# Three merges of a two-block transformer: per branch four gates and four products twice, or eight gates and then eight products

## The chip, the cores and the metric

The kernel runs on one core of a Trainium2 chip. Its time is the device time of one execution, in microseconds (us). The core's engines are TensorE (PE in the profile, its weight loads PEld), VectorE (DVE), ScalarE (ACT), GpSimd (POOL) and SyncE (SP), which issues the loads of the weight stream. Each engine runs its own list of instructions in order; they meet only by semaphores.

## What is computed

Two transformer blocks, one after the other, on 256 tokens of width 1024, in float32. The parts that matter are the merges of the branches. The first block merges four branches of width 1024:

```python
gates = jax.nn.sigmoid(proj("gates").reshape(b, s, N_BRANCH, D_MODEL) + b_gate[l])
projected = jnp.einsum('bsnc,ncd->bsnd', branches, w_branch[l])
mixed = jnp.sum(gates * projected, axis=2)
x = x + mixed @ w_out[l]
```

The second block has two layers, and each merges three branches of width 512 (neighbourhood attention, differential attention, gMLP). Its first layer carries 256 tokens of x and 256 of the context together, 512 columns; its last layer only the 256 of x:

```python
def branch_merge(ya, yb, yc, gates, w_branch, w_out):
    ga, gb, gc = jnp.split(jax.nn.sigmoid(gates), N_BRANCH_2, axis=-1)
    m = ga * (ya @ w_branch[0]) + gb * (yb @ w_branch[1]) + gc * (yc @ w_branch[2])
    return m @ w_out
```

Behind each layer of the second block comes a mixture of 16 experts whose weights stream past.

## The kernel before

Activations lie with features on partitions and tokens in columns. A dense projection makes one output chunk of 128 features in one PSUM bank, by the sum over eight (or, in the second block's products, four) input chunks. The weights arrive as one stream in **pieces** of 128 x 1024 numbers, two to a slot of a ring of six (`ring`). Float32 is multiplied in split form: `split_hi` (L498, on ACT) rounds a piece to its high part, `split_lo` (L507 on VectorE, L509 on POOL) subtracts to get the low part, and `three` (L605 to L607) does three matmuls per block, high by high, high by low and low by high. A piece gives 24 matmuls. Which pieces' low parts POOL makes is a table, `GPS_LOW`. Both halves of the split run up to `AHEAD` = 3 pieces in front of TensorE, held back by the `piece_used` semaphores; in program text they hang on `next_piece`, which every engine calls as it passes a piece (`split_ahead`).

The program is a list of stages with a `barrier` between them (L485, semaphore `stage_done`): every engine drains, signals, and waits for four signals. POOL makes its low parts in `lows`, in the stage in which ACT made the high parts.

A **merge** (`merge_pe`, `merge_act`, `merge_dve`) goes branch by branch. ACT rounds the branch's y (L1816) and VectorE subtracts (L1848); TensorE waits for that (`y_lo`) before its first product. Then, for each half h of the eight output chunks: TensorE makes four gate banks, from the activations in `A`, and four product banks, from y in `WKR`. ACT turns each gate bank into `GATE` by a sigmoid (L1820); VectorE multiplies `GATE` with each product bank (L1857) and adds it into `MIXT` (L1859). `GATE` has room for four chunks of 512 columns, so at the start of every half ACT waits for `gate_used`, which VectorE gives, after a drain, at the end of a half. A first-block piece makes one bank of either kind; in the second block a piece makes one gate bank or two product banks. Banks come from a ring of six in the first merge and of eight in the others. In the first merge conditioning steps (`ada_pe`, L2019) on unsplit pieces follow every second piece.

At the end of a merge the mix itself is split for the out projection (`out_pe`): ACT makes the high part of a chunk (`mix_hi_act`, L1800), POOL the low part (`mix_lo_pool`, L1805), and the first bank of the out projection takes all eight chunks in turn, waiting for each. In the last half of the last branch ACT does chunks 0 to 3 right behind the gates and chunks 4 to 7 as VectorE finishes them.

Ahead of a second-block merge lies the gMLP stage. It ends with transposes on TensorE, copied by ACT (`gmlp_mix_act`, L2279); then ACT loads the table for the sigmoid (`table`, L1035: a tiny activation that makes the load happen), and the barrier follows. The stage's gelu is L2230. Before it lies the differential attention (`att_pe`, `att_act`, `att_dve`), during which the gMLP's projections and the splits of the first merge pieces are made; L944 is VectorE's weighting of the two attention maps. Ahead of the first merge lies memory attention, `mem_att`, in two rounds.

## Time and profile before

| | before |
|---|---|
| time, median of 3 runs | 2789.27 us (2784.52 to 2792.49) |
| time of the profiled execution | 2788.38 us |
| its span | 2786.4 us |
| TensorE busy | 2534.9 us |
| VectorE busy | 1044.3 us |
| ACT busy | 880.5 us |
| POOL busy | 424.2 us |
| high parts of pieces (L498) | 378, 393.1 us |
| low parts on VectorE (L507) | 255, 316.5 us |
| low parts on POOL (L509) | 123, 312.7 us |
| mean granted clock of TensorE | 0.98 of full |

The busy times are sums over the whole span; each engine's work lies partly beside the others'. A wait costs time only where TensorE, or the stream of expert weights that later fills the span, stands still for it. So the table says how much work there is, and the rows below say where it is waited for.

### The profile page before, as it was taken

To read this page: it belongs to the slowest core of one execution; us is meant where nothing else is said; L and a number is where in the kernel's file an instruction comes from. 1 tells how busy PE (TensorE), PEld (TensorE's weight loads), DVE (VectorE), ACT (ScalarE), POOL (GpSimd) and SP (SyncE) were. 2 spreads that over 40 slices of the span, in tenths; PEclk is the share of its full clock that TensorE was granted. 3 is DMA by queue.
4 is the path that set the end of the run, shared out by engine and by line. 5 is a ranking of instruction groups with operands and counts; after the bars stand their busy time and mean duration, and the time that the engine had idled before them with its cause. 6 is when DMAs were issued, how large, how long until landed. Compare 5 with 4: busy or idle time off the path is not lost.

```text
span 2786.4 us, 36544 instructions
## 1 busy us (share of the span) xinstructions
PE 2534.9 (91%) x15220; PEld 1805.0 (65%) x15220; DVE 1044.3 (37%) x1528; ACT 880.5 (32%) x1392; POOL 424.2 (15%) x222
## 2 busy tenths in 40 slices
PE   7999989999999999899999888888999998987787
PEld 7888878899998777688863222224777895322223
DVE  4548532326764444544441011113474653000001
ACT  4465544344444344422331100002344442000001
POOL 1430016771001232100220000000133011000000
PEclk9999999999999999899999999999999999999999
DMA  5434327764544221323269999999213448999997
GB/s 211 157 137 153 119 77 280 299 240 174 185 156 152 76 72 46 151 91 121 96 265 397 429 428 429 429 429 377 101 61 133 152 151 361 425 429 429 429 430 316
DMA packets 66510, 668.27 MB, mean 240 GB/s; under 512 B 7328, under 2 KB 8496, under 8 KB 10544
## 3 DMA queue, kind: packets, MB, share of 16 engines
q1 hardware_dynamic: 64368, 655.48, 59.2%
q0 software_dynamic: 1984, 10.51, 1.0%
q8 instruction: 121, 1.98, 0.3%
q14 instruction: 37, 0.30, 0.0%
HBM read 664.89 MB, written 1.06 MB: 239 GB/s over the span
## 4 chain that ended last, share of the span: by engine, by line
PE 54%; DMA 22%; DVE 5%; ACT 3%; issue 2%; PEld 2%; POOL 1%; DVEq 0%; POOLq 0%; PEldq 0%; ACTq 0%
PE ps L605 12%; PE ps L607 12%; PE ps L606 12%; DMA ring<-in_blocks 10%; PE ps L2508 9%; DMA hi_place<-in_blocks 7%; DMA WK<-in_blocks 5%; PE ps L825 1%; PE ps L2019 1%; PE ps L794 1%; POOL A L1805 1%; PE ps L633 1%; PE ps L811 1%; PE ps L613 1%; ACT WK L869 1%
## 5 line engine op out<-in xcount | busy, mean ns | idle before, releaser
L605 PE MATMUL ps<-A,piece_hi 128*128 128x256 f32 (+1 forms) x1952 | 617.8, 316 | 19.7 <-ACTq L485 7.2
L606 PE MATMUL ps<-A,piece_hi 128*128 128x256 f32 (+1 forms) x1952 | 605.2, 310 | 0.0
L607 PE MATMUL ps<-A,ring_lo 128*128 128x256 f32 (+1 forms) x1952 | 604.7, 310 | 0.0
L498 ACT ACTIVATE piece_hi<-ring 128x1024 fp32r<-128x1024 f32 x378 | 393.1, 1053 | 202.0 <-DVEq L644 104.8
L509 POOL TENSOR_TENSOR ring_lo<-ring,piece_hi 128x1024 fp32r<-128x1024 f32 x123 | 312.7, 2554 | 680.2 <-ACT piece_hi L498 622.5
L605 PEld LDWEIGHTS ps<-A,piece_hi 128*128 128x128 f32 x1952 | 377.4, 193 | 58.2 <-issue 24.7
L507 DVE TENSOR_TENSOR ring_lo<-ring,piece_hi 128x1024 fp32r<-128x1024 f32 x255 | 316.5, 1246 | 253.7 <-ACT piece_hi L498 253.2
L606 PEld LDWEIGHTS ps<-A,piece_hi 128*128 128x128 f32 x1952 | 377.9, 194 | 17.8
L607 PEld LDWEIGHTS ps<-A,ring_lo 128*128 128x128 f32 x1952 | 377.5, 193 | 18.1
L2659 DVE TENSOR_TENSOR A_place<-A_place,ps 128x512 f32<-128x512 f32 x32 | 22.0, 688 | 539.4 <-PE ps L2508 539.4
L1047 POOL TENSOR_TENSOR WK<-WK 128x512 f32<-128x512 f32 (+1 forms) x36 | 40.5, 1125 | 1025.5 <-ACT WK L1041 1024.8
L605 PE MATMUL ps<-WKR,piece_hi 128*128 128x256 f32 (+1 forms) x624 | 188.1, 302 | 1.0 <-DVE WKR L726 0.8
L606 PE MATMUL ps<-WKR,piece_hi 128*128 128x256 f32 (+1 forms) x624 | 186.7, 299 | 0.0
L607 PE MATMUL ps<-WKR,ring_lo 128*128 128x256 f32 (+1 forms) x624 | 186.7, 299 | 0.0
L2625 ACT ACTIVATE A_place<-ps 128x512 f32<-128x512 f32 x32 | 19.1, 597 | 495.9 <-PE ps L2508 495.9
L2508 PE MATMUL ps<-ring,A_place 128*64 128x512 f32 x672 | 152.2, 597 | 18.7 <-ACT A_place L2631 13.0
L2508 PE MATMUL ps<-ring,WK 128*64 128x512 f32 x656 | 148.3, 596 | 19.5 <-DMA ring<-in_blocks 19.5
L605 PE MATMUL ps<-piece_hi,A 128*128 128x256 f32 (+1 forms) x480 | 156.2, 325 | 2.5 <-DVE WK L2121 2.3
L607 PE MATMUL ps<-piece_hi,A 128*128 128x256 f32 (+1 forms) x480 | 152.9, 318 | 0.0
L606 PE MATMUL ps<-ring_lo,A 128*128 128x256 f32 (+1 forms) x480 | 152.8, 318 | 0.0
L2508 PE MATMUL ps<-WK 128*64 128x512 f32 x512 | 116.0, 596 | 24.6 <-DMA WK<-in_blocks 24.6
L2608 DVE COPY WK<-ps 32x512 f32<-32x512 f32 x48 | 32.7, 682 | 260.0 <-PE ps L2508 259.8
(295 smaller groups left out, 3283.6 us busy)
## 6 DMA issues: line engine op xcount, KB each, us to landing
ring<-in_stream SPq DMA_DIRECT2D x237, 1024.0 KB, 4.9
ring<-in_blocks SPq DMA_DIRECT2D x82, 2048.0 KB, 25.1
WK<-in_blocks SPq DMA_DIRECT2D x39, 2048.0 KB, 25.6
extra<-in_blocks SPq DMA_DIRECT2D x28, 2048.0 KB, 25.6
hi_place<-in_blocks SPq DMA_DIRECT2D x28, 2048.0 KB, 25.6
A_place<-in_blocks SPq DMA_DIRECT2D x11, 2048.0 KB, 34.6
WK<-in_na_bias POOLq DMA_DIRECT2D x2, 2048.0 KB, 8.0
WK<-in_blocks SPq DMA_DIRECT2D x4, 1024.0 KB, 28.3
```

What stands on the lines that cost most here:

```text
L498: nc.scalar.activation(piece_hi[:, no % 4, :], ring[:, slot, at:at + PIECE], ACT.Copy).then_inc(hi_done[no % 4], 1)
L507: nc.vector.tensor_tensor(to, of, hi, ALU.subtract).then_inc(lo_done[no % 4], 1)
L509: nc.gpsimd.tensor_tensor(to, of, hi, ALU.subtract).then_inc(lo_done[no % 4], 1)
L605: nc.tensor.matmul(out_, l[0], r[0], start=first, stop=False)
L606: nc.tensor.matmul(out_, l[0], r[1], start=False, stop=False)
L607: return nc.tensor.matmul(out_, l[1], r[0], start=False, stop=last)
L613: nc.tensor.matmul(out_.rearrange("p (a t) -> p a t", a=2), ident, ident.unsqueeze(1).to_broadcast([P, 2, P]), start=True, stop=True)
L633: last = nc.tensor.matmul(ps[0:rows, b, at:at + n], l, r, start=(k == 0), stop=(k == len(pairs) - 1))
L794: last = nc.tensor.matmul(dst[:, a, qt, :], l, m, start=(j == 0), stop=(j == len(pairs) - 1))
L1047: ins = nc.gpsimd.tensor_tensor(sq[:, 0, 0:n], sq[:, 0, 0:n], sq[:, c, 0:n], ALU.add)
L2508: last = nc.tensor.matmul(ps[64 * n:64 * n + 64, bank, :].rearrange("p (a t) -> p a t", a=2), lhs, block_half(pe, layer, b, k % 4, n), sta ...
L2608: return copy(YE[row:row + CAP, s, e // 4 % 2, half * 512:half * 512 + 512], ps[64 * half + CAP * s:64 * half + CAP * (s + 1), 6 + e % 2, :])
```

## The change

In all three merges a branch now does its eight gates and then its eight products. The order of the weight stream follows, as do the three engines' programs. The room for gates doubles: with 256 columns both halves fit in `GATE`, with 512 a second place, `LATER_GATE`, is used. ACT waits for `gate_used` once per branch, and before it splits chunks 0 to 3 of the mix. Beside this:

- the table load for the sigmoid comes ahead of the gMLP copies (`table` before `gmlp_mix_act`);
- `GPS_LOW` has the first three merge pieces of both layers of the second block, before only those of the first layer;
- memory attention puts its products into banks 0 to 3 instead of 6 and 7;
- a table `GATES_AHEAD` allows gates ahead of a merge; all its values are 0.

```diff
+GATES_AHEAD = {"first": 0, 0: 0, 1: 0}
...
-                   (block + 32, block + 35)):
+                   *((block + l * layer + 32, block + l * layer + 35 + GATES_AHEAD[l]) for l in range(LAYERS))):
...
-                if at["y_bank"] < 6:
+                if at["y_bank"](r) == 4:
                     pe.wait_ge(att_saved, CREDIT + base + r)
...
-            return (YT[:, 3, 4 * r:4 * r + 4, :].rearrange("p (b c) t -> p b (c t)", b=2), ps[:, 6:8, :])
+            return (YT[:, 3, 4 * r:4 * r + 4, :].rearrange("p (b c) t -> p b (c t)", b=2), ps[:, 2 * r:2 * r + 2, :])
...
+        LATER_GATE = wk(16640, 4, 2 * T)
...
+        def gate_at(n, h, j):
+
+            if n == T:
+                return GATE[:, j, h * T:(h + 1) * T]
+            return (GATE, LATER_GATE)[h][:, j, :]
...
             for i in range(branches):
-                for h in range(2):
-                    for _ in range(2):
-                        two_pieces(in_a()(n), DC)
-                    if h == 0:
-                        pe.wait_ge(y_lo, cur.base("y") + 1 + i)
-                    for _ in range(kc // 4):
-                        two_pieces(lambda k: (yh[:, k, :], yl[:, k, :]), kc)
+                for _ in range((8 - (0 if i else ahead)) // 2):
+                    two_pieces(in_a()(n), DC)
+                pe.wait_ge(y_lo, cur.base("y") + 1 + i)
+                for _ in range(2 * kc // 4):
+                    two_pieces(lambda k: (yh[:, k, :], yl[:, k, :]), kc)
...
+            for i in range(branches):
+                act.wait_ge(gate_used, cur.base("merge") + 1 + i * 2)
+                nc.scalar.activation(yh, y[:, i, :, 0:n], ACT.Copy).then_inc(y_hi, 1)
+                for c in range(0 if i else ahead, DC):
+                    gate_act(act, cur, i, c, n, bias)
                 for h in range(2):
...
                     last = (i, h) == (branches - 1, 1)
                     if last:
+                        act.wait_ge(gate_used, cur.base("merge") + 2 + i * 2)
                         for c in range(4):
                             mix_hi_act(c, n)
...
+                for _ in range((8 - (0 if i else ahead)) // 2):
+                    skip_fm(dve, cur, 2)
+                    behind_two()
+                gates_end = cur.g
                 for h in range(2):
-                    for _ in range(2):
-                        skip_fm(dve, cur, 2)
-                        behind_two()
-
-                    dve.wait_ge(bank_free[cur.bank(cur.g - 1)], cur.bank_use(1, cur.g - 1))
+                    if h == 0:
+                        dve.wait_ge(bank_free[cur.bank(gates_end - 1)], cur.bank_use(1, gates_end - 1))
...
-                gmlp_mix_act(act, cur, n // P)
                 table(steps, ACT.Sigmoid)
+                gmlp_mix_act(act, cur, n // P, layer)
                 barrier(act, cur)
```

The first place is ACT at the end of the gMLP stage of the second block's first layer. In these rows L2279 and L2308 are the copies, L1035 and L1039 the table, L1816 and L1831 the first operation of the merge. Before:

```order
L498 ACTIVATE piece_hi<-ring 128x1024 [waits piece_used3,landed5]
L498 ACTIVATE piece_hi<-ring 128x1024 [waits piece_used0,landed0]
L2279 ACTIVATE WK<-ps 128x4x128 [waits bank_full3]
L2279 ACTIVATE WK<-ps 128x4x128 [waits bank_full4]
L2279 ACTIVATE WK<-ps 128x4x128 [waits bank_full5]
L2279 ACTIVATE WK<-ps 128x4x128 [waits bank_full0]
L1035 ACT_TABLE_LOAD
L1035 ACTIVATE idle<-idle 128x1
L1816 ACTIVATE WKR<-WK 128x2048 [waits act_step,gate_used,stage_done]
```

And with the change:

```order
L501 ACTIVATE piece_hi<-ring 128x1024 [waits piece_used3,landed5]
L501 ACTIVATE piece_hi<-ring 128x1024 [waits piece_used0,landed0]
L1039 ACT_TABLE_LOAD
L1039 ACTIVATE idle<-idle 128x1
L2308 ACTIVATE WK<-ps 128x4x128 [waits bank_full3,act_step]
L2308 ACTIVATE WK<-ps 128x4x128 [waits bank_full4]
L2308 ACTIVATE WK<-ps 128x4x128 [waits bank_full5]
L2308 ACTIVATE WK<-ps 128x4x128 [waits bank_full0]
L1831 ACTIVATE WKR<-WK 128x2048 [waits gate_used,stage_done]
```

The load moved from behind the four copies to ahead of them; there is still one load.

The second place is ACT in the last branch of that layer's merge. L1820 and L1824 are sigmoids of gate banks, L498 and L501 high parts of pieces, L1800 and L1812 high parts of the mix. Before:

```order
L1820 ACTIVATE WK<-ps 128x512 [waits bank_full2]
L498 ACTIVATE piece_hi<-ring 128x1024 [waits piece_used1,landed4]
L1820 ACTIVATE WK<-ps 128x512 [waits bank_full3]
L498 ACTIVATE piece_hi<-ring 128x1024 [waits piece_used2,landed5]
L1800 ACTIVATE A<-WK 128x512 x4
L498 ACTIVATE piece_hi<-ring 128x1024 [waits piece_used3,landed5]
L1800 ACTIVATE A<-WK 128x512 [waits bank_free4]
```

And with the change:

```order
L1824 ACTIVATE WK<-ps 128x512 [waits bank_full7]
L501 ACTIVATE piece_hi<-ring 128x1024 [waits piece_used0,landed4]
L501 ACTIVATE piece_hi<-ring 128x1024 [waits piece_used1,landed4]
L501 ACTIVATE piece_hi<-ring 128x1024 [waits piece_used2,landed5]
L1812 ACTIVATE A<-WK 128x512 [waits gate_used]
L1812 ACTIVATE A<-WK 128x512 x3
L501 ACTIVATE piece_hi<-ring 128x1024 [waits piece_used3,landed5]
L1812 ACTIVATE A<-WK 128x512 [waits bank_free4]
```

The last gates lie four product banks further back, and the first high part of the mix has got a wait for `gate_used`.

The third place is POOL's whole order in the last layer, up to the split of the mix (L1805, L1817). L509 and L512 are low parts of pieces. Before:

```order
L509 TENSOR_TENSOR ring_lo<-ring,piece_hi 128x1024 x15
L3192 DMA WK<-in_w_s 128x512
L3193 DMA WK<-in_ln_g 128x512
L3194 DMA WK<-in_ln_b 128x512
L509 TENSOR_TENSOR ring_lo<-ring,piece_hi 128x1024 x5
L1805 TENSOR_TENSOR A<-WK,A 128x256 x8
```

And with the change:

```order
L512 TENSOR_TENSOR ring_lo<-ring,piece_hi 128x1024 x15
L3224 DMA WK<-in_w_s 128x512
L3225 DMA WK<-in_ln_g 128x512
L3226 DMA WK<-in_ln_b 128x512
L512 TENSOR_TENSOR ring_lo<-ring,piece_hi 128x1024 x8
L1817 TENSOR_TENSOR A<-WK,A 128x256 x8
```

Three low parts have come to POOL's list ahead of the gMLP stage; VectorE's list has three fewer.

## Rows read from the trace of the kernel before

**Rows 1.** The table by stretch, one row per merge of the program.

```profile
413.67:634.70 221.03, 219.88 (x1774) 196.19 (x1774) 73.14 (x78) 89.49 (x109) 159.28 (x70) 0.99 0.72 266
1179.42:1385.00 205.58, 204.58 (x889) 168.79 (x890) 89.71 (x88) 60.34 (x72) 14.26 (x8) 0.99 0.29 103
2174.43:2285.00 110.57, 109.01 (x885) 108.13 (x885) 68.08 (x88) 50.71 (x72) 8.96 (x8) 0.98 0.49 172
```

**Rows 2.** TensorE's waits over the span (us, times, longest), then timeline at merges' edges.

```profile
PE ps L605 <- ACTq L485: 7.2, 3, 2.7
PE ps L605 <- POOL A L1805: 3.6, 5, 1.0
...
1179.42 0.79 PE L605 MATMUL ps<-A,piece_hi 128*128 128x512 f32 x1 [2.24 <-ACTq L485]
1384.13 0.50 PE L605 MATMUL ps<-A,piece_hi 128*128 128x512 f32 x1 [1.00 <-POOL A L1805]
2174.43 0.39 PE L605 MATMUL ps<-A,piece_hi 128*128 128x256 f32 x1 [2.24 <-ACTq L485]
```

**Rows 3.** Groups by line in the first merge, then ACT's timeline near its end.

```profile
L509 POOL TENSOR_TENSOR ring_lo<-ring,piece_hi 128x1024 fp32r<-128x1024 f32 x61 | 150.2, 2479 | 91.1 <-ACT piece_hi L498 91.0
L1859 DVE TENSOR_TENSOR WK<-WK 128x256 f32<-128x256 f32 x32 | 41.4, 1293 | 1.1
L1816 ACT ACTIVATE WKR<-WK 128x2048 fp32r<-128x2048 f32 x4 | 7.7, 1914 | 12.9 <-DVEq L1863 10.5 <-DVEq L1844 2.4
...
616.23 0.47 ACT L1820 ACTIVATE WK<-ps,par 128x256 f32<-128x256 f32 x1 [1.46 <-PE ps L607]
619.11 0.47 ACT L1820 ACTIVATE WK<-ps,par 128x256 f32<-128x256 f32 x1 [1.46 <-PE ps L607]
```

**Rows 4.** Timeline of VectorE in the last merge, two successive product pieces.

```profile
2190.32 0.42 DVE L1857 TENSOR_TENSOR WK<-WK,ps 128x256 f32<-128x256 f32 x1
...
2193.04 0.42 DVE L1857 TENSOR_TENSOR WK<-WK,ps 128x256 f32<-128x256 f32 x1
```

**Rows 5.** Timeline of ACT at the end of the two gMLP stages.

```profile
1174.11 0.60 ACT L2279 ACTIVATE WK<-ps 128x512 f32<-128x512 f32 x1 [8.66 <-PE ps L631]
...
1177.83 1.28 ACT L1035 ACT_TABLE_LOAD   x1
...
2172.84 1.28 ACT L1035 ACT_TABLE_LOAD   x1
```

**Rows 6.** The table by stretch, the first 4 us of the second merge.

```profile
1179.40:1183.40 4.00, 3.98 (x9) 3.14 (x10) 3.11 (x1) 0.00 (x0) 0.00 (x0) 0.50 0.00 0
```

**Rows 7.** Timelines of VectorE and ACT, differential attention of the last layer.

```profile
2136.31 3.53 DVE L944 SCALAR_TENSOR_TENSOR WK<-WK,small 128x512 f32<-128x512 f32 x2
...
2149.29 1.41 DVE L944 SCALAR_TENSOR_TENSOR WK<-WK,small 128x512 f32<-128x512 f32 x2
...
2155.34 1.05 ACT L498 ACTIVATE piece_hi<-ring 128x1024 fp32r<-128x1024 f32 x1
...
2158.27 1.15 ACT L2230 ACTIVATE WK<-WK 128x512 f32<-128x512 f32 x2
```

**Rows 8.** Timelines of ACT, VectorE and POOL at the ends of both later merges.

```profile
1367.61 0.60 ACT L1820 ACTIVATE WK<-ps 128x512 f32<-128x512 f32 x1 [3.89 <-PE ps L607]
...
1369.18 1.23 DVE L507 TENSOR_TENSOR ring_lo<-ring,piece_hi 128x1024 fp32r<-128x1024 f32 x1 [4.21 <-ACT piece_hi L498]
...
1369.81 14.26 POOL L1805 TENSOR_TENSOR A<-WK,A 128x512 fp32r<-128x512 f32 x8 [193.58 <-ACT A L1800]
...
2275.99 8.96 POOL L1805 TENSOR_TENSOR A<-WK,A 128x256 fp32r<-128x256 f32 x8 [133.91 <-ACT A L1800]
```

**Rows 9.** Timelines of VectorE, POOL and ACT, last branch of the first merge.

```profile
605.19 2.52 DVE L1859 TENSOR_TENSOR WK<-WK 128x256 f32<-128x256 f32 x1
...
620.61 4.97 POOL L509 TENSOR_TENSOR ring_lo<-ring,piece_hi 128x1024 fp32r<-128x1024 f32 x2 [0.47 <-ACT piece_hi L498]
...
621.65 2.00 ACT L498 ACTIVATE piece_hi<-ring 128x1024 fp32r<-128x1024 f32 x2
```

More of the change, by code:

```diff
@@ L142, in steps @@
                     ADA_LAST[ada_step(part, slot)[:2]] = at - 1
-    steps(0, range(32), 2)
+    at += GATES_AHEAD["first"]
+    steps(0, range((64 - GATES_AHEAD["first"]) // 2), 2)
     at += BLOCK_PIECES - 22 * 4 - 64
@@ L824, in product @@
                         for rows, col, pairs in parts[at_:at_ + width]:
-                            last = nc.tensor.matmul(ps[rows, at["y_bank"] + col // 512, col % 512:col % 512 + T], *pairs[j],
+                            last = nc.tensor.matmul(ps[rows, at["y_bank"](r) + col // 512, col % 512:col % 512 + T], *pairs[j],
                                                     start=(j == 0), stop=(j == kc - 1))
@@ L2204, in build, with gates_ahead_of_tile @@
         GST = wk(18688 + 1536, 4, 8)
+        def gates_ahead_of_tile(layer, m, tt):
+            n = GATES_AHEAD[layer]
+            return (m + 1) * n // tt - m * n // tt
         def gmlp_pe(pe, cur, tt, layer, lam_init):
@@ L2887, in _ @@
             cur.set_ring(range(6))
-            merge_pe(pe, cur, 4, DC, T, ada=0)
+            merge_pe(pe, cur, 4, DC, T, GATES_AHEAD["first"], ada=0)
             cur.set_ring(range(NB))
@@ L2925, in _ @@
                 cur.set_ring(range(NB))
-                merge_pe(pe, cur, 3, BC, n)
+                merge_pe(pe, cur, 3, BC, n, GATES_AHEAD[layer])
                 out_pe(pe, cur, n)
@@ L2992, in _ @@
             cur.set_ring(range(6))
-            merge_act(act, cur, 4, DC, T, YT, lambda i, c: p1("b_gate", i * DC + c))
+            merge_act(act, cur, 4, DC, T, YT, GATES_AHEAD["first"], lambda i, c: p1("b_gate", i * DC + c))
             cur.set_ring(range(NB))
@@ L3087, in _ @@
             cur.set_ring(range(6))
-            merge_dve(dve, cur, steps, 4, DC, T, YT, ada=0)
+            merge_dve(dve, cur, steps, 4, DC, T, YT, GATES_AHEAD["first"], ada=0)
             cur.set_ring(range(NB))
@@ L3273, in _stream @@
     tm(x["w_mem_kv"][0], D, 2 * D)
+    two = -(GATES_AHEAD["first"] // 2)
     for n in range(4):
-        for h in range(2):
-            for j, w, at in ((0, w_in, g0 + n * D), (1, w_in, g0 + n * D), (2, x["w_branch"][0, n], 0), (3, x["w_branch"][0, n], 0)):
-                at += h * 512 + j % 2 * 256
-                fm(w, at, at + 256)
-                ada(0, 8 * n + 4 * h + j)
+        for w, at in ((w_in, g0 + n * D), (x["w_branch"][0, n], 0)):
+            for j in range(4):
+                fm(w, at + j * 256, at + j * 256 + 256)
+                if two >= 0:
+                    ada(0, two)
+                two += 1
     fm(x["w_out"][0], 0, D)
```

64 lines of the change are left out of this document (38 added, 26 removed).

## The prediction, made before the changed kernel was run

> **What bounds the kernel now.** The change removes no matmul, so it pays only where TensorE stands still. First the table by stretch: the three merges lie at 413.67 to 634.7, 1179.42 to 1385.0 and 2174.43 to 2285.0 us, and TensorE is busy for 219.88 of 221.03, 204.58 of 205.58 and 109.01 of 110.57 us of them [rows 1]. Then the list of TensorE's waits over the whole span: the split matmuls of L605 waited three times for ACT at a stage's end, 7.2 us, and five times for POOL's low parts of the mix, 3.6 us [rows 2]. The timeline puts 2.24 us before each second-block merge and 1.00 us at the end of the first of these two [rows 2]; the first merge's start has the other 7.2 - 4.5 = 2.7 us. Between gates and products, or from branch to branch, there is no wait at all. So what the edit reorders is covered, and all it can win at the merges' edges is 7.2 + 3.6 = 10.8 us, 0.39% of 2788.38. I take 0.3%, 8.4 us, as what a measurement of this kernel can tell from no change.
>
> **Part 1: gates and products.** The counts stay: per branch eight gates and eight products on TensorE, eight sigmoids on ACT, eight multiplies and adds on VectorE, the same pieces of weights in a new order of the stream. At 256 columns a piece takes 619.11 - 616.23 = 2.88 us, the distance of two gates [rows 3]. Removed are ACT's wait and VectorE's hand-over between the halves; both lie under TensorE's work, 0 us. What covers them is the splitting of weights ahead: ACT makes a piece's high part up to three pieces early, and POOL or VectorE its low part.
> In the first merge POOL takes 2.48 us a piece, and 61 low parts fill 150.2 of 221 us [rows 3]: it keeps up in either order. In the last merge VectorE has low parts and products: the pairs of multiply and add of two banks and one low part go round in 2193.04 - 2190.32 = 2.72 us [rows 4], under 2.88, so it does not fall behind in four product pieces in a row either. With 512 columns a piece lasts about twice as long. Cost 0 us; the upper bound is rival B.
>
> **Part 2: the sigmoid table ahead of the copies.** ACT idles 8.66 us before its gMLP copies, then copies, then loads the table, and only then reaches the stage's end. The load starts at 1177.83 and TensorE at 1179.42; in the last layer 2172.84 and 2174.43 [rows 2, 5]. With the load inside the idle time TensorE starts about 0.1 us after the last copy: 1.59 - 0.1 = 1.5 us won, twice, **-3.0 us**. Bounds: 0, should the load come again for the first sigmoid or another engine hold the stage, and -3.0.
> The Trainium skill, page "ScalarE: Activation LUTs", section "What ACT_TABLE_LOAD costs", puts a switch to another set at 1.28 us for the load and 1.38 us of draining, 2.66 us together. By that the two would give 5.3 in place of 3.0 and the sum would be 2.3 us lower. The trace agrees with 1.28 for the load and shows TensorE started 1.59 after the load began, so no such drain is there to win.
>
> **Part 3: the clock at these starts.** From 1179.4 to 1183.4 the granted clock was 0.50, the 1.2 GHz level, after TensorE had stood still [rows 6]; 4 us at half speed cost 2 us. A shorter gap may keep the clock up (-2, and as much in the last layer), or only shift the fall (0). Nothing in the rows says at what point of the gap it fell, so I take 0 and keep both ends.
>
> **Part 4: three low parts go from VectorE to POOL in the last layer.** They are the first three merge pieces, made during the differential attention; POOL's order has 8 low parts there in place of 5. ACT's last high part starts at 2155.34 and ends at 2156.39. POOL's low part of 2.48 us then ends at about 2158.9, and POOL must reach that stage's end before ACT's gelu can start, which it did at 2158.27 [rows 7]. Cost **+0.6 us**. Bounds: 0, and +2.1: beside POOL's low parts VectorE's pair of L944 took 3.53 us, alone 1.41 [rows 7], and TensorE turns the result of that chain. Against it VectorE is rid of low parts of 1.23 us ahead of the same chain, so I take the first value, the nearest row.
> The Trainium skill, page "GPSIMD Engine Reference", section "1. Specifications", says that GpSimd and VectorE share SBUF interfaces and contend when a VectorE instruction has two SBUF inputs. The rows of L944 agree. By that rule alone this part would cost 2.1 us and the sum be 1.5 higher.
>
> **Part 5: the end of each merge.** This is the part that can cost. ACT rounds chunks 0 to 3 of the mix, POOL subtracts, and the first bank of the out projection needs all eight. Before, ACT did it right behind the last gate's sigmoid and a high part. Now, at the same point of TensorE's work, it waits for `gate_used`, which VectorE gives after its fourth product and the low part queued behind that. So the price is (multiply and add, low part, hand-over) less (sigmoid, high part).
> Second merge: POOL made its eight subtractions without a pause in 14.26 us from 1369.81, and TensorE waited 1.00 us for the last [rows 2, 8], so POOL's start sets the end. Before: sigmoid 0.60 and high part 1.05, less their overlap, 1.5. Now: a pair at 256 columns is half of 2.72 - 1.23, 0.75, so 1.4 or so at 512, then 1.23 and 0.1, 2.7. **+1.2 us**.
> Last merge, 256 columns: before 0.47 at most and 1.05, about 1.4; now 0.75 + 1.23 + 0.3 = 2.3. POOL again ran without a pause, from 2275.99 [rows 8]. **+0.9 us**.
> First merge: POOL first finishes two low parts, begun at 620.61, the second from a high part that was ready at about 622.7 [rows 9]. In the new order products don't hold ACT, the earlier of the two comes a piece sooner, and POOL waits for the second alone: it begins at 622.7 in place of 620.61 + 2.48 = 623.1. **-0.4 us**.
> Bounds: 0 for each of the three, and twice the value, or +1 for the first.
>
> **Part 6: memory attention's banks.** Its products go to banks 0 to 3 in place of 6 and 7; all its waits remain, and those banks' scores are read by then. 0 us. `GATES_AHEAD` is zero for all three merges, so the code for gates ahead issues nothing.
>
> **Sum:** -3.0 + 0 + 0.6 + 1.2 + 0.9 - 0.4 = **-0.7 us** against the profiled execution's 2788.38 (span 2786.4), which is 0.9 below the median of 2789.27; on the median 2788.6 us. All favourable ends: -3.0 - 4.0 + 0 + 0 - 0.8 = -7.8. All unfavourable: 0 + 0 + 2.1 + 2.4 + 1.8 + 1.0 = +7.3. Independent parts don't all fall one way; about half of each, -4.5 and +4.
>
> **Rivals.**
> A, faster: the edges close, clock included. For it speaks that the clock was at half at the second merge's start. If parts 2 and 3 give all (-7.0) and TensorE's waits for POOL go too (-3.6), with part 4 at +0.6, it is -10.0: 2779.3. Against it: the chain at the merges' ends gets longer, not shorter. 6%.
> B, slower: VectorE falls behind in the eight products of the first merge, and the next branch starts late. POOL's low parts do hold VectorE's adds: one took 2.52 us, and the mean is 1.29 [rows 3, 9]. From TensorE's last product to the low part of the next branch's fourth piece the chain is multiply 0.42, add 2.52, copy of y 1.91, sigmoid 0.47, high part 1.05, low part 2.48 [rows 3, 4, 7, 9], 8.85 us, and TensorE needs 3 x 2.88 = 8.64 for three gates. It decides where VectorE is a whole further piece behind, 2.9 us. At one and a half, 4.3, three starts lose 4.3 + 0.2 each, 13.5 us: 2802. Against it: 0.42 + 2.52 = 2.94 is only 0.06 over a piece even at the worst. 8%.
> C, the change does not do at the edges what it says: the table is loaded again, or POOL holds the stage. Part 2 gives 0, -0.7 + 3.0: 2791.6. 8%.
> D, the clock stays up at one or both starts: -2 to -4 more, 2784.6 to 2786.6. 8%.
> The forecast has the remaining 70%.
>
> **How the numbers follow.** The forecast, C and D lie within 8.4 us of 2789.3: 86% for the same; A is the 6% for faster, B the 8% for slower. The runs shown spread from 2784.52 to 2792.49 around their median, and I allow 1.5 us for a median of such runs. Range: 2788.6 - 4.5 - 1.5 = 2782.6, and 2788.6 + 4 + 1.5 = 2794, to 2795 for the nearest part of B. It takes in C and D and leaves out A and B, 14%.
>
> **What would show it.** Part 2: ACT's table load ahead of the gMLP copies, and the merge's first matmul 1.5 us sooner after the last copy. Part 4: POOL's low part ends after 2158.27, measured from ACT's last high part, and the gelu follows it. Part 5: a wait near 2 us in place of 1.00 behind the second merge. A wait of L605 inside a merge would mean B. The forecast is wrong if the merges' edges keep their waits and the time still moves, or if waits appear where now there is none.

## The result and the profile after

The changed kernel took 2792.99 us (median of 20 runs, 2790.73 to 2795.41), the kernel before 2788.35 in 20 runs on the same chip: ratio 1.0017, 95% interval 1.001 to 1.0023. So it is slower, by 2.8 to 6.4 us, where 0.7 us less was forecast. The profiled execution has a span of 2790.8 us against 2786.4.

First TensorE's waits in the changed kernel, by releaser (us in total, times, longest), which answer to [rows 2]:

```profile
PE ps L1240 <- ACT WK L1261: 5.9, 2, 4.9
PE ps L608 <- POOL A L1817: 4.8, 9, 1.2
PE ps L608 <- ACTq L488: 4.1, 3, 2.7
```

And the wait for the gelu's chain (two of them, the last layer's is the longer) in the kernel before:

```profile
PE ps L1236 <- ACT WK L1257: 5.4, 2, 4.1
```

The merges' starts lost 7.2 - 4.1 = 3.1 us of waits, as forecast. The waits at the merges' ends grew by 4.8 - 3.6 = 1.2 us (1.0, 1.0 and 1.6 at the three ends before, 1.5, 1.5 and 1.7 now), and the wait for the gelu's chain in the last layer 4.9 - 4.1 = 0.8. The waits named here come to -3.1 + 1.2 + 0.8 = -1.1 us, so none of the 4.4 us of the spans is explained by them. The table by stretch tells more: columns are the stretch, its length, busy time of TensorE, its weight loads, VectorE, ACT and POOL, then TensorE's granted clock (1.00 is the 2.4 GHz level), DMA share and GB/s. In the changed kernel, the three merges, then 3.4 us behind the first merge's end and 3.3 behind the second's:

```profile
415.09:635.84 220.75, 219.23 (x1768) 195.52 (x1768) 68.61 (x78) 89.88 (x109) 157.89 (x68) 0.99 0.72 267
1181.24:1385.00 203.76, 202.24 (x889) 166.69 (x890) 89.12 (x88) 60.48 (x72) 13.89 (x8) 1.00 0.29 104
2178.66:2288.00 109.34, 107.53 (x885) 106.51 (x885) 67.78 (x88) 50.83 (x72) 8.15 (x8) 1.00 0.49 174
637.00:640.40 3.40, 3.33 (x16) 3.25 (x16) 1.55 (x2) 1.37 (x2) 0.78 (x2) 0.51 0.46 140
1384.70:1388.00 3.30, 3.30 (x10) 2.54 (x9) 2.00 (x3) 1.58 (x2) 0.00 (x0) 0.51 0.00 0
```

And the same two places of the kernel before:

```profile
635.60:639.00 3.40, 3.40 (x31) 3.40 (x30) 2.09 (x4) 1.90 (x3) 0.00 (x0) 1.00 0.75 292
1385.00:1388.30 3.30, 3.30 (x16) 2.72 (x15) 2.01 (x3) 1.58 (x2) 0.00 (x0) 1.00 0.00 0
```

The bodies of the merges are as before [rows 1], with no new wait between or inside branches. But behind both ends the granted clock is now 0.51, about 1.2 GHz: TensorE starts 16 matmuls in the time of 31, and 10 in the time of 16, and stays "busy" all the while. Such stretches let its busy time grow, from 2534.9 to 2539.1 us in all, at the same 15220 matmuls. Behind the last merge it is the other way round. The kernel before, then the changed one:

```profile
2284.30:2287.70 3.40, 3.38 (x15) 3.29 (x16) 1.54 (x2) 1.37 (x2) 0.65 (x1) 0.53 0.00 0
```

```profile
2288.15:2291.55 3.40, 3.33 (x28) 3.26 (x28) 1.61 (x2) 1.37 (x2) 0.08 (x1) 1.00 0.02 5
```

**A ledger over all profiles.** Every kernel of this study runs those 15220 matmuls in the same stages, so the time between the starts of the same two of them (counted from the first) compares kernels, waits and clock together. In us; "body" stretches inside the merges are alike in all (212.4, 185.87, 93.60) and left out. The columns: up to the first merge's start (1st to 2631st matmul); its end (4361st to 4401st); from there past the second merge's start (to 7961st); the second merge's end (8781st to 8861st); layer 0's experts and layer 1's attention (to 12281st); past the last merge's start (to 12421st); from the last merge's end on (13201st to the last; it has the last merge's end in it). The names other than before and after are the kernels below.

| kernel | begin | 1st end | 2nd start | 2nd end | between | last start | rest |
|---|---|---|---|---|---|---|---|
| before | 407.70 | 6.71 | 557.13 | 19.47 | 755.16 | 31.53 | 501.46 |
| before_again | 406.83 | 6.75 | 553.69 | 19.47 | 755.17 | 31.52 | 502.20 |
| after | 408.90 | 9.22 | 552.19 | 21.87 | 757.63 | 30.40 | 503.10 |
| after_again | 409.64 | 9.23 | 552.43 | 21.90 | 757.12 | 30.41 | 501.26 |
| banks_back | 407.85 | 9.13 | 552.39 | 21.91 | 757.21 | 30.41 | 503.50 |
| low_back | 409.92 | 9.11 | 552.36 | 21.92 | 757.79 | 28.29 | 502.39 |
| table_only | 412.24 | 6.73 | 551.24 | 19.47 | 757.62 | 31.23 | 502.01 |
| order_only | 412.22 | 9.11 | 555.60 | 20.30 | 756.19 | 33.03 | 501.85 |
| high_first | 409.72 | 5.55 | 551.53 | 20.29 | 757.56 | 30.18 | 506.41 |
| late_round | 411.82 | 6.71 | 553.60 | 21.21 | 753.82 | 31.89 | 504.75 |
| chunk_first | 411.49 | 5.55 | 553.83 | 20.29 | 754.40 | 30.42 | 501.83 |
| chunk_second | 410.79 | 9.22 | 552.47 | 18.13 | 758.00 | 32.61 | 504.30 |
| chunkwise | 406.92 | 5.56 | 552.24 | 18.13 | 754.47 | 30.41 | 502.02 |
| chunk_low | 410.22 | 5.59 | 551.59 | 18.13 | 756.36 | 31.27 | 502.20 |

The mean of the two profiles of the changed kernel, less the mean of the two of before: begin +2.0, 1st end +2.5, 2nd start -3.1, 2nd end +2.4, between +2.2, last start -1.1, rest +0.4; together +5.3, near the 4.6 of the medians. The first end repeats within 0.15 us where nothing touches it. The second end takes one of two values at the same waits: about 21.9 with a fall of the clock behind it, 20.3 without. The outer columns swing by several us from one execution to the next: "begin" lies between 406.83 and 412.24 in before, before_again, table_only and late_round, which are one program up to there. So a single profile can't carry a verdict there.

Two places that the wide columns hide, counted in the same way: the second merge's first matmuls (7911th to 7961st) and the last merge's end (13201st to 13290th).

| kernel | second merge's start | last end |
|---|---|---|
| before | 14.28 | 14.84 |
| before_again | 14.24 | 14.85 |
| after | 11.45 | 14.13 |
| after_again | 11.45 | 14.11 |
| table_only | 13.36 | 14.94 |
| order_only | 13.07 | 14.82 |
| chunkwise | 11.44 | 13.69 |

With these the ledger parts as follows. Where the change acts, the changed kernel is not slower in these profiles: 1st end +2.5, 2nd end +2.4, last end -0.7, second merge's start -4.3 (1.5 of wait and 2.8 of clock), last start -1.1, together -1.2. The other +6.5 us lie where it changes little or nothing: begin +2.0, between the first end and the second merge +1.2, between +2.2, behind the last end +1.1. Two profiles of each kernel can't tell how much of that is swing. So that the ends got dearer is plain in the ledger; that they are what makes the whole kernel slower has to come from the experiments.

### The profile page after: what moved, and what is told of

It is laid out like the page before. It is cut to its first block, busy times and chain, and to the rows that moved or that the text cites. A ratio compares the mean times of both kernels' runs of the same rounds, so it can differ in the third digit from the quotient of the medians.

```text
span 2790.8 us, 36540 instructions
## 1 busy us (share of the span) xinstructions
PE 2539.1 (91%) x15220; PEld 1806.0 (65%) x15220; DVE 1037.5 (37%) x1525; ACT 881.4 (32%) x1392; POOL 431.4 (15%) x225
## 4 chain that ended last, share of the span: by engine, by line
PE 53%; DMA 22%; DVE 6%; ACT 3%; issue 2%; PEld 2%; POOL 2%; DVEq 0%; POOLq 0%; PEldq 0%; ACTq 0%
PE ps L608 12%; DMA WK<-in_blocks 12%; PE ps L610 12%; PE ps L609 12%; DMA ring<-in_blocks 10%; PE ps L2537 9%; PE ps L2035 1%; PE ps L797 1%; PE ps L828 1%; POOL A L1817 1%; PE ps L636 1%; PE ps L814 1%; ACT WK L872 1%; PE ps L616 1%; DVE small L933 1%
## 5 line engine op out<-in xcount | busy, mean ns | idle before, releaser
L501 ACT ACTIVATE piece_hi<-ring 128x1024 fp32r<-128x1024 f32 x378 | 393.8, 1054 | 229.6 <-DVEq L647 126.6
L512 POOL TENSOR_TENSOR ring_lo<-ring,piece_hi 128x1024 fp32r<-128x1024 f32 x126 | 320.8, 2557 | 689.9 <-ACT piece_hi L501 632.8
```

Of the source, the lines that this page charges most:

```text
L501: nc.scalar.activation(piece_hi[:, no % 4, :], ring[:, slot, at:at + PIECE], ACT.Copy).then_inc(hi_done[no % 4], 1)
L512: nc.gpsimd.tensor_tensor(to, of, hi, ALU.subtract).then_inc(lo_done[no % 4], 1)
```

## What holds the merges' ends

**The first merge.** ACT and then POOL in the changed kernel at its end:

```profile
617.68 1.06 ACT L501 ACTIVATE piece_hi<-ring 128x1024 fp32r<-128x1024 f32 x1 [1.82 <-DVEq L647]
623.28 1.34 ACT L1812 ACTIVATE A<-WK 128x256 fp32r<-128x256 f32 x4 [4.54 <-DVEq L1879]
624.52 1.99 ACT L501 ACTIVATE piece_hi<-ring 128x1024 fp32r<-128x1024 f32 x2
...
610.51 12.40 POOL L512 TENSOR_TENSOR ring_lo<-ring,piece_hi 128x1024 fp32r<-128x1024 f32 x5 [0.47 <-ACT piece_hi L501]
625.64 2.42 POOL L512 TENSOR_TENSOR ring_lo<-ring,piece_hi 128x1024 fp32r<-128x1024 f32 x1 [2.73 <-ACT piece_hi L501]
628.00 9.11 POOL L1817 TENSOR_TENSOR A<-WK,A 128x256 fp32r<-128x256 f32 x8
```

ACT stands 4.54 us at its wait for `gate_used` (L1879 gives it). Queued behind that wait is the high part of the piece whose low part is POOL's last. POOL therefore stands 2.73 us and starts the eight subtractions of the mix at 628.00. In the kernel before:

```profile
625.54 9.09 POOL L1805 TENSOR_TENSOR A<-WK,A 128x256 fp32r<-128x256 f32 x8
```

Against TensorE's position that is 628.00 - 1.42 - 625.54 = 1.0 us later than before (1.42 us is how late the changed kernel was at the 4321st matmul).

**The second merge.** TensorE's two longest waits there, and POOL:

```profile
1382.75 0.50 PE L608 MATMUL ps<-A,piece_hi 128*128 128x512 f32 x1 [1.25 <-POOL A L1817]
1383.98 0.50 PE L608 MATMUL ps<-A,piece_hi 128*128 128x512 f32 x1 [0.27 <-POOL A L1817]
...
1370.04 13.89 POOL L1817 TENSOR_TENSOR A<-WK,A 128x512 fp32r<-128x512 f32 x8 [190.47 <-ACT A L1812]
```

The changed kernel was 1.0 us ahead here, so POOL started 1370.04 + 1.0 - 1369.81 = 1.2 us later, which is the forecast's number. The clock's fall behind it was not in the forecast.

## The experiments

Four were made first, to part the change into its pieces and mend the place suspected.

**table_only**, the kernel before with one line moved:

```
+                table(steps, ACT.Sigmoid)
                 gmlp_mix_act(act, cur, n // P)
-                table(steps, ACT.Sigmoid)
```

> The kernel before, with nothing changed but the sigmoid table's load put ahead of the gMLP copies. Theory 1 (the change wins at the starts of the second-block merges and loses more at the merges' ends): TensorE's three waits for ACT's queue go from 7.2 us to about 4.1, the ends keep 3.6 us of waits for POOL, and the granted clock at the start of the second merge stays up as in the changed kernel, 1.7 to 3.4 us more: 3.0 to 6.4 us below the kernel before, ratio 0.9977 to 0.9989. Theory 2 (the table move itself does harm, or its gain is given back at the next wait): ratio 0.9995 or more.

2787.56 us against 2789.5: ratio 0.9991 (0.9981 to 1.0). Faster by some 2 us, at the edge of what can be told from nothing, and short of the 3.0 to 6.4 expected. The waits for ACT's queue did go to 4.1. But at the second merge's start the clock did not stay up, as theory 1 had it: it was at half until 4.0 us behind the first matmul, and the start took 13.36 us, against 14.28 before and 11.45 in the changed kernel. So the move of the table alone does not free that start from the half clock. In the last layer the clock took most of the won time back. Around the start, in this kernel (the first matmul of the merge is at 2174.48, 1.6 us into the window) and from the start in the kernel before:

```profile
2172.90:2179.60 6.70, 5.97 (x28) 5.58 (x29) 2.99 (x2) 1.83 (x3) 0.00 (x0) 0.50 0.01 2
```

```profile
2174.43:2178.00 3.57, 3.57 (x20) 3.57 (x21) 1.90 (x2) 1.06 (x1) 0.00 (x0) 0.62 0.02 5
```

TensorE waits 1.5 us less and starts 1.1 us sooner against the 12281st matmul, since the transposes ahead ran at the lower level too; then it spends more of its work at that level, and the column "last start" is only 0.3 us shorter.

**order_only**, the reverse: the changed kernel without the table's move, the three low parts and the banks.

> The kernel before with the order of gates and products changed in all three merges, and neither the table's move, nor the three low parts on POOL, nor the other banks of the memory attention. Theory 1: the waits at the merges' ends are 4.8 us or more, those at their starts 7.2 us again, and the half-clock stretch at the second merge's start is back: 2 to 6 us above the changed kernel, 2795 to 2799. Theory 2 (the order costs nothing; the loss is in the other parts): 2789 to 2790, as the kernel before.

2798.72 us, ratio 1.0036 (1.0023 to 1.0049), from 5 runs. It is 9.2 us slower than the kernel before, twice as much as the whole change; theory 2 is out. The size is not well known: it stands on five runs, and of the 9 us by which the profile is longer, 5 lie in "begin", where the program is that of the kernel before. Its waits are as theory 1 had them, 7.2 and 4.8 us. At the second merge's start the half clock is back, as expected (13.07 us). At its second end the waits alone stand in the ledger: 20.30, 0.83 over the kernel before, with no fall of the clock. With the fall it is 21.9.

**low_back**:

```
-                   *((block + l * layer + 32, block + l * layer + 35 + GATES_AHEAD[l]) for l in range(LAYERS))):
+                   (block + 32, block + 35)):
```

> The changed kernel with the last layer's first three merge pieces given back to VectorE for their low parts. Theory 1: the wait for the gelu's input in the last layer goes from 4.9 back to about 4.1 us, 0.5 to 1.0 us below the changed kernel, 2792 to 2792.5. Theory 2 (this part is what made the kernel slower): 3 to 5 us below it, 2788 to 2790.

2791.5 us, ratio 1.0013 (1.0004 to 1.0023). The gelu's wait is 4.1 again, as theory 1 had it; the time is 1.5 lower than the changed kernel's, a little more than expected and inside the intervals. This part is not the loss.

**chunkwise**, the mend. In the last branch of each merge ACT no longer waits once for four chunks:

```
-                for h in range(2):
-                    last = (i, h) == (branches - 1, 1)
-                    if last:
-                        act.wait_ge(gate_used, cur.base("merge") + 2 + i * 2)
-                        for c in range(4):
-                            mix_hi_act(c, n)
...
+                for c in range(DC):
+                    read_bank(act, cur, False, None, piece=(kc == DC or c % 2 == 1))
+                    if i == branches - 1 and c > 0:
+                        act.wait_ge(bank_free[cur.bank(cur.g - 2)], cur.bank_use(1, cur.g - 2))
+                        mix_hi_act(c - 1, n)
```

> The changed kernel, but in the last branch of each merge ACT rounds each chunk of the mix behind the product piece after it, in place of four chunks behind one wait for VectorE. Theory 1 (the loss sits at the merges' ends): POOL starts its subtractions earlier, TensorE's 4.8 us of waits for POOL's low parts of the mix fall below 1.5 us, and the half-clock stretches of 3.4 us behind the first and the second merge are gone (1.7 us each): 4 to 7 us below the changed kernel, 2786 to 2789. Theory 2 (the loss sits in the last layer's attention, with the three low parts that went to POOL): no more than 2 us below it, 2791 to 2793.

2785.75 us, 7 us under the changed kernel; against before 0.999 (0.9978 to 1.0002). Both ends fall under the kernel before: 5.56 and 18.13. The half-clock rows behind both are gone. Of the waits for POOL 2.7 us are left, more than the 1.5 expected: 0.5 at the first end, none at the second, and 2.2 at the last, where the last chunks' roundings come two by two with a piece between and POOL's last pair is late. Against TensorE's position the last end is still 0.4 us shorter than in the changed kernel (13.69 and 14.13). Theory 2 allowed 2 us at most. Nothing but the rounding at the ends was edited, and the loss was gone; but both ends went below the kernel before, so some of the 7 us was never lost.

Then the same place was taken apart.

**high_first**: in the first merge alone, ACT makes the next high part before that wait.

```
+                    if last and kc == DC:
+                        read_bank(act, cur, False, None, piece=True)
                     if last:
                         act.wait_ge(gate_used, cur.base("merge") + 2 + i * 2)
...
-                        read_bank(act, cur, False, None, piece=(kc == DC or j % 2 == 1))
+                        if not (last and kc == DC and j == 0):
+                            read_bank(act, cur, False, None, piece=(kc == DC or j % 2 == 1))
```

> The changed kernel, but at the end of the first merge ACT makes the high part of the next piece of weights before it waits for VectorE's fourth product, not behind it. Theory 1 (that high part, held behind ACT's wait, leaves POOL idle for 2.73 us before its last low part, and its eight subtractions of the mix start late): POOL's pause falls below 0.6 us, the subtractions start about 2.5 us earlier, TensorE's stretch at the first merge's end is 2.5 us shorter (1.2 of wait, 1.3 of half clock): 2790 to 2791 if the changed kernel is 2793. Theory 2 (POOL's start is set by the roundings themselves): the stretch stays within 0.3 us.

ACT and POOL in this kernel:

```profile
621.52 1.06 ACT L501 ACTIVATE piece_hi<-ring 128x1024 fp32r<-128x1024 f32 x1 [2.10 <-DVEq L647]
623.98 1.34 ACT L1812 ACTIVATE A<-WK 128x256 fp32r<-128x256 f32 x4 [1.40 <-DVEq L1882]
...
611.20 14.97 POOL L512 TENSOR_TENSOR ring_lo<-ring,piece_hi 128x1024 fp32r<-128x1024 f32 x6 [0.48 <-ACT piece_hi L501]
626.12 7.45 POOL L1817 TENSOR_TENSOR A<-WK,A 128x256 fp32r<-128x256 f32 x7
634.38 1.19 POOL L1817 TENSOR_TENSOR A<-WK,A 128x256 fp32r<-128x256 f32 x1 [0.81 <-ACT A L1812]
```

POOL's six low parts now follow one another without the pause. The subtractions start 2.6 us earlier (this kernel was 0.7 us behind the changed one there: 628.00 + 0.7 - 626.12), and the end falls from 9.22 to 5.55 us, by more than the 2.5 expected: one high part held behind one wait was worth 3.7 us at that place, clock included. The whole kernel took 2791.36 us (1.0008, 0.9998 to 1.0018), 1.6 under the changed kernel, a difference that the intervals don't secure; "rest" was 3 to 5 us longer in this profile.

**chunk_first**, the rounding by chunks in the first merge alone (`if kc == DC`):

> The changed kernel with the rounding chunk by chunk in the first merge alone. Theory 1: the stretch at the first merge's end falls by 3.6 us against the changed kernel, as in the kernel with all three (there 1.15 under the kernel before), the second and last merges stay as in the changed kernel: 2789 to 2790.5. Rival (the three ends are not additive, since an end that is mended gives the clock back elsewhere): 2786 or 2792.

2791.03 us, ratio 1.001 (1.0001 to 1.0019): half a microsecond over the range. The first end is 5.55, 3.7 less, as expected. The second was expected as in the changed kernel and is 20.29: the same waits of 1.25 and 0.27 us, but no fall behind them. high_first has 20.29 too. Both kernels differ from the changed one in the first merge alone, so whether the clock falls at the second end is not settled by the waits there.

**chunk_second**, in the two later merges alone (`if kc == BC`):

> The changed kernel with the rounding chunk by chunk in the two second-block merges alone. Theory 1 (the clock falls behind longer waits, and the second merge's end brings the larger part of the lost clock, since with the first merge alone mended the mean granted clock stayed at 0.980): TensorE's stretch at the second merge's end is 3.7 us shorter than in the changed kernel, the mean granted clock is 0.981 or more, 2787 to 2789. Rival (the parts don't show singly; only all three ends together raise the clock): 2790 to 2792 and 0.980.

2788.76 us, ratio 0.9998 (0.9988 to 1.0007), within the expected 2787 to 2789. The ends are 9.22 and 18.13, 3.7 below the changed kernel at the second, as expected. The mean granted clock over its 11 runs is 0.9806, just short of 0.981. The two halves, 2.0 and 4.2 us, come to 6.2 of the 7.2 that all three ends gave.

**late_round**, the kernel before in its own order, with the first four roundings put later:

```
-                    if last:
-                        for c in range(4):
-                            mix_hi_act(c, n)
                     for j in range(4):
                         read_bank(act, cur, False, None, piece=(kc == DC or j % 2 == 1))
+                        if last and j == 0:
+                            act.wait_ge(bank_free[cur.bank(cur.g - 1)], cur.bank_use(1, cur.g - 1))
+                            for c in range(4):
+                                mix_hi_act(c, n)
```

> The kernel before, in its own order of gates and products, but in each merge's last half ACT rounds the first four chunks behind VectorE's first product there, in place of right behind the last gate: the price of a later start of POOL's subtractions, by itself. Theory 1 (a later start is what the reordering costs, and it draws the clock with it): POOL starts 2 to 3 us later at the second and the last merge, TensorE's waits for POOL go from 3.6 to 7 to 9 us, the mean granted clock falls by 0.001 to 0.002, 5 to 9 us above the kernel before, 2794 to 2799. Rival (only the wait counts, the clock does not follow): 2 to 4 us above.

2793.97 us against 2789.21, ratio 1.002 (1.001 to 1.003). POOL started at 1373.39 and 2279.80:

```profile
PE ps L605 <- POOL A L1805: 5.5, 8, 1.2
...
1373.39 13.31 POOL L1805 TENSOR_TENSOR A<-WK,A 128x512 fp32r<-128x512 f32 x8 [196.71 <-ACT A L1800]
```

A late start of POOL alone, in the old order, makes the kernel slower by 4.8 us, about as much as the change did. But neither theory was met: the waits grew by 1.9 and not by 3.4 or more, since POOL went through its eight in 13.31 in place of 14.26 us, and the mean granted clock fell by 0.0005 (0.9820 to 0.9815), no more than the error of its 11 runs. The second end is 1.7 longer and the last end 1.8 (16.67 against 14.85), with no half-clock row right behind the second end.

**banks_back**, memory attention's products in banks 6 and 7 again:

```
-            cur.set_ring((6, 7))
             att_pe(pe, cur, mem_att)
...
-            return (YT[:, 3, 4 * r:4 * r + 4, :].rearrange("p (b c) t -> p b (c t)", b=2), ps[:, 2 * r:2 * r + 2, :])
+            return (YT[:, 3, 4 * r:4 * r + 4, :].rearrange("p (b c) t -> p b (c t)", b=2), ps[:, 6:8, :])
```

> The changed kernel with the memory attention's products in banks 6 and 7 again, as before the change. Theory 1 (this part costs nothing): the stretch up to the first merge keeps its waits and the time is within 1.5 us of the changed kernel, 2791.5 to 2794.5. Rival (the order of the banks costs a wait or a clock fall ahead of the first merge): 2788 to 2790.

2792.7 us, ratio 1.0014 (1.0005 to 1.0023): as the changed kernel. This part costs nothing.

**before_again** and **after_again**, both kernels unchanged for second profiles:

> The kernel before, unchanged, for a second profile of it. Theory 1 (the clock's short falls come at TensorE's waits, but not in the same ones in every execution): the waits at the merges' starts and ends repeat within 0.3 us, and the half-clock stretches differ from the first profile in 3 or more places, most of all in the stages that the change does not touch. Rival (the falls are fixed by the program): the same stretches at the same places. Time 2788 to 2790, ratio 0.999 to 1.001.

2789.87 us, 1.0002 (0.9993 to 1.0012). The waits repeat: 7.2 and 3.6 us at the merges' edges. The clock's falls don't: "2nd start" differs by 3.4 us between the two profiles of one kernel, and the first has several half-clock rows that the second lacks. Over the whole execution the first was granted 0.980 of the clock and the second 0.984.

> The changed kernel once more, for a second profile. Theory 1: 2792 to 2794, mean granted clock 0.980 against 0.982 of the kernel before; half-clock stretches again behind the first and the second merge, other places move. Rival (the first 20 runs were high by chance): 2789 to 2790.5.

2792.65 us, 1.0012 (1.0003 to 1.0022), with the falls behind both ends again (9.23 and 21.90). The slower result is no chance.

**chunk_low**, chunkwise rounding and the three low parts back on VectorE:

> The changed kernel with the rounding chunk by chunk in all three merges, and the last layer's three low parts back on VectorE. Theory 1: the gains add up: the waits at the merges' ends are gone, the gelu's input waits 4.1 in place of 4.9 us, 1.5 to 2 us below the kernel with chunkwise rounding alone, 2783 to 2785, and faster than the kernel before by 3 to 6 us. Rival (below the level of the kernel with only the table moved nothing is left to win): 2786 to 2788.

2782.94 us against 2789.65, ratio 0.9976 (0.9967 to 0.9986): 6.7 us faster than the kernel before and about 10 faster than the change as made. TensorE's waits and POOL at the second merge's end, in this kernel:

```profile
PE ps L1240 <- ACT WK L1261: 4.7, 2, 4.1
PE ps L608 <- ACTq L488: 4.1, 3, 2.7
PE ps L608 <- POOL A L1817: 2.8, 4, 1.0
...
1357.46 1.29 POOL L1817 TENSOR_TENSOR A<-WK,A 128x512 fp32r<-128x512 f32 x1 [181.10 <-ACT A L1812]
1376.46 1.55 POOL L1817 TENSOR_TENSOR A<-WK,A 128x512 fp32r<-128x512 f32 x1 [1.30 <-ACT A L1812]
```

The 2.8 us are 0.5 at the first end, none at the second, 2.2 at the last. In the second merge POOL starts some 9 us earlier against TensorE's position (this kernel was 3.2 us ahead of the changed one there) and is done at 1378.0; TensorE no longer waits for it. The old order can't do this, since the rounded mix goes into the tile that the second half's gates still read. So the new order is an advantage at the ends, once the rounding uses it: the first end is 1.2 and the second 1.3 us shorter than before. The rest of the 6.7 us is not parted; the moved table load is in it too.

## Why the prediction was wrong

The point was 2788.6 and the result 2792.99, in the range, but with the sign against it; "slower by over 0.3%" was not reached either.

**Part 5, the ends of the merges, is the step that failed, and with it the clock, for which the sum had no term behind the ends.** It forecast +1.2 (second), +0.9 (last) and -0.4 (first merge), with bounds of 0 and twice the value, or +1 for the first; together +1.7. Measured from matmul to matmul: +2.4, -0.7 and +2.5, together +4.2. Each parts into waits and clock:

- Second end: 0.8 is waits (20.3 in the three kernels in which the clock did not fall there), 1.6 the clock.
- First end: the lag behind the kernel before grows from 1.42 to 2.47 us up to the 4386th matmul, so the waits and the slow starts behind them cost 1.05; from there on at half clock 1.46 more are lost.
- Last end: the waits cost 0.5 (the 13222nd matmul comes 5.53 us behind the 13201st, before 4.99). POOL started 1.1 us later and took 8.38 us for its eight in place of 8.96 [rows 8]. But the kernel before had a fall of the clock behind this end, in both profiles, and the changed kernel has none.

By waits alone the three come to 2.4 us where 1.7 was forecast. Even that is near by luck: an end forecast as a gain was a loss, and the two others were over-sized (the hand-over in them, 0.1 and 0.3 us, came from no row).

- In the first merge the mechanism itself was wrong. "it begins at 622.7", the forecast said, from a high part that would be ready as before [rows 9]. But ACT's queue is in order: the high part stands behind the new wait for `gate_used`. I had counted that wait's price for the mix and not for what is queued behind it. high_first shows it: that high part put ahead of the wait, and the end is 3.7 us shorter.
- In the second merge the wait was a little over-sized (1.2 for 0.8, since POOL took 13.89 in place of 14.26 us for its eight) and the clock behind it left out. A gap of 1.0 us before [rows 2] left the clock at 1.00; 1.25 and 0.27 us, with smaller ones about them, were followed by 0.51 in four profiles (after, after_again, banks_back, low_back) and not in three (order_only, high_first, chunk_first). The forecast looked at the clock only where TensorE had been still for 2.24 us.

That the rounding at the ends is worth this much is shown by the mends: all three ends edited gave 7.2 us back, the first alone 2.0, the two others 4.2. It is not shown that the ends are the whole loss. In chunkwise the places that the change touches are 9.1 us shorter than before (ends -1.2, -1.3 and -1.2, second start -4.3, last start -1.1), and the kernel gained only 2.8 us by the ratio and 3.8 by the medians. So there as in the changed kernel some 6 us are lost at places that the change leaves alone; which ones and why stays open.

**Part 3, the clock at the starts**, was put at 0 with bounds of -4 and 0. At the second merge's start it is full in all four profiles that keep the unmended change (for instance from 1181.20, below), where it was at half before [rows 6]. That is worth 2.8 us there (14.26 to 11.45), more than the 2 that the bound had, and is what rival D named. Neither the table's move alone (13.36) nor the order alone (13.07) gave it. Yet "2nd start" as a whole fell by 3.1 us on the mean of two, and by 1.3 against before_again: the falls move among stages ahead of it. So D's condition came true at one start, and the time that it forecast did not follow. In the last layer table_only gave most of the won 1.5 back. To "only shift the fall", the other case that the forecast named, is what it did there.

```profile
1181.20:1185.20 4.00, 3.96 (x17) 3.30 (x18) 3.11 (x1) 0.00 (x0) 0.00 (x0) 1.00 0.00 0
```

**Part 2, the table**, held: waits 7.2 to 4.1 us, 1.5 at each start, no second load. The Trainium skill's 2.66 us per switch (page "ScalarE: Activation LUTs", section "What ACT_TABLE_LOAD costs") would have taken 5.3 off; the traces disagree, 3.1 went.

**Part 4, three low parts to POOL**, forecast +0.6, was +0.8 to +0.9 (4.9 against 4.1 in the lists, 4.95 against 4.06 in the timelines): POOL's last low part, and ACT's gelu waiting for POOL. In the changed kernel:

```profile
2160.32 2.34 POOL L512 TENSOR_TENSOR ring_lo<-ring,piece_hi 128x1024 fp32r<-128x1024 f32 x1 [3.78 <-ACT piece_hi L501]
...
2163.02 1.15 ACT L2253 ACTIVATE WK<-WK 128x512 f32<-128x512 f32 x2 [0.90 <-POOLq L488]
```

With the clock it is more in place ("last start" is 2.1 us shorter in low_back), but the whole kernel gained 1.5 at most by undoing it.

**Part 1 and part 6** held at 0: the bodies of the merges agree to 0.1 us, so rival B, VectorE falling behind in eight products, did not occur, and banks_back is as the changed kernel. Rival C failed with part 2. Rival A did not occur; chunk_low reached 6.7 of its 10.0 us, with a mend that A did not name.

**The clock as a whole.** The mean granted clock over all timed runs is 0.9801 for the changed kernel (20 runs, and 10 more) and 0.9817 to 0.9820 for the kernel before (29 and twice 33 runs). One less the clock, times the time, is what TensorE would make up at full clock if it were always busy: 2793 x 0.0199 = 55.6 against 2789 x 0.0183 = 51.0 us. The difference, 4.6 us, is as large as the result, but it is an upper bound and not a measurement. The two profiles of the kernel before had 0.980 and 0.984, 11 us by this reckoning, and their spans differ by 2.8 (2786.4 and 2783.6), so time at half clock is not all lost time. Among the runs of one kernel 0.001 of clock goes with about 1.7 us (a line fitted through all of them), which makes about 3 of the 4.6 us. That is an estimate; the rest stays open. With all ends mended the clock is 0.9822 and 0.9818; with the first alone 0.9800 and 0.9803; with the last two ends alone 0.9806; with the low parts or the banks alone undone 0.9799 and 0.9797; in order_only, over 5 runs, 0.9790; in table_only and late_round 0.9815.

What stays open: the 6.5 us of the ledger outside the edges of the merges. About 2 of them lie between the second merge's end and layer 1's gelu, which the change touches in three pieces at most. Those pieces are not the reason: low_back, without them, has 757.79 there, and table_only, which does not reorder anything, 757.62. In the changed kernel the clock was at half in these two stretches of layer 1's attention, and at full at the same places before. Ahead of the first of them TensorE had stood 2.26 us for VectorE, before 2.27. The changed kernel, then the kernel before:

```profile
2080.90:2084.30 3.40, 3.40 (x18) 3.40 (x18) 3.33 (x2) 0.00 (x0) 3.09 (x2) 0.50 0.00 0
2118.40:2121.80 3.40, 3.40 (x9) 1.20 (x6) 3.35 (x3) 0.45 (x1) 2.56 (x1) 0.50 0.38 148
```

```profile
2078.80:2082.20 3.40, 3.40 (x31) 3.40 (x30) 3.36 (x2) 0.00 (x0) 3.17 (x2) 1.00 0.00 0
2115.30:2118.70 3.40, 3.04 (x14) 1.63 (x10) 3.37 (x4) 0.02 (x1) 2.57 (x1) 1.00 0.25 100
```

That a shift of the program by a microsecond decides whether such a wait draws the clock down is my reading; no run here tests it. Nor is it settled why the gains of the single ends come so unevenly in the clock.

## What to carry to other kernels

When a change makes an in-order engine wait at a new place, price everything queued behind that wait, above all the pieces that another engine's last task needs, and let the engine wait chunk by chunk for what it handles chunk by chunk. Price a wait of TensorE with the granted clock behind it, and read the clock in the stretch after each wait that grows, since "busy" hides it. An order of work that looks neutral can still be worth having for what it allows at the edges: measure it with the edge rewritten to use it. And where the same program differs by several us from one profile to the next, take a second profile of both kernels before a stretch is blamed.

## What the runs showed of the hardware that was not expected

- Waits of 1.25 and 0.27 us just ahead were followed by 3.3 us at 0.51 of the clock in four profiles and by no fall in three; 1.00 us was not followed by one. At the last merge's end 1.6 us of waits were followed by a fall in both profiles of the kernel before, and 1.7 us by none in both of the changed kernel. Two waits of 2.27 and 2.26 us at the same place of the program ended one with the clock at full, the other at half. So the length of the wait alone does not decide.
- The fall costs twice what the wait's growth did: at the second end 0.8 us of wait alone (20.30 against 19.47) and 2.4 with the fall (21.9).
- POOL's subtraction of a 128x512 chunk took 1.29 us in chunk_low where VectorE had little to do beside it, 1.55 where it had a low part or an add, and 13.89 / 8 = 1.74 in a row at the end of the merge. The Trainium skill, page "GPSIMD Engine Reference", section "1. Specifications", tells of SBUF interfaces that GpSimd shares with VectorE; these rows agree. The same eight took 11.4 us of POOL's time spread out and 13.89 in a row.
